# One attention block stack and one recurrent block stack in a single launch: a unit's matrices moved to memory of their own, steps reordered around them, and extra idle-time matmuls

## The chip, the cores and the metric

The kernel runs on one core of one Trainium2 chip. The metric is the device time of one execution in microseconds; the time of a kernel is the median of several runs. The profile comes from one further execution.

## The reference, cut to what matters

The program computes two transformer-like blocks in float32 on one sequence of 256 tokens and a width of 1024. The first block (two layers of three attention branches and an MLP) is not touched by the change. The second block begins with an "even mixer", which is where every edit lies:

```
q, k, v = silu(conv(x @ w_in))            # gated delta rule: 4 heads of 128
g, beta = gates(x @ w_in)
o  = gated_delta_chunked(q, k, v, g[0], beta[0]) + flip(gated_delta_chunked(flip(q), ...))
y_dn = rms_norm(o, dn_norm) * silu(dn_gate)

r, k, v, w_f, w_b, a = ...                # RWKV-7: 8 heads of 64
y  = rwkv7_scan(r, w_f, k, v, -kk, kk * a) + flip(rwkv7_scan(flip(...)))
y_rk = (group_norm(y) * ln_w + ln_b + bonus) * silu(rk_gate)

h = layer_norm(ALPHA * h + concat(y_dn, y_rk) @ w_out, ln_g, ln_b)
h = h + sigmoid(h @ ple_gate) * rms_norm(p @ ple_w, ple_norm)
```

Both recurrences are computed in chunks of 128 tokens in the kernel. A chunk needs a triangular inverse, three dependent products with it ("solve"), and a state that is handed to the next chunk; each recurrence runs once forward and once backward.

## The kernel before, in words

Each engine has a program written out by hand, and the functions of one stage are named after it: `..._tensor` runs on PE, `..._vector` on DVE, `..._scalar` on ACT, `..._gpsimd` on POOL, `..._sync` on SP, which issues all loads. Within an engine the order is the order of the calls. Engines wait for named events (`("xt", tag, i)`); an event that an engine has passed is not waited for again.

Dense products take weights in pieces of 128 x 2048. SP loads a piece, ACT rounds it (`high_of_next`, two instructions at L353), DVE makes the remainder (`low_of_next`, two instructions at L366), and PE multiplies three times (L390, L391, L392). A `Filler` is a list of steps from another stage, of which one is put between two steps of the current one.

The gated delta rule (`delta_tensor`, `delta_vector`, `delta_scalar`) goes over both directions d and in each over two chunks (step 0 and 1). A step is: kS (L2087, needs the state), the right-hand side on DVE, three solve products (L2192) with an ACT copy after the first and the second (L3195) and a DVE subtraction after the third (L2665), then o and kU or qS (L2087). `claim(..., warm=n)` takes a PSUM bank and puts n products of the identity with itself (L281, two instructions each) ahead of the wait for the operands; they compute nothing that is used.

RWKV runs as four units: (d, step) = (0,0), (0,1), (1,0), (1,1), called unit 0 to 3 here. In the text of the code, the pass n of `rwkv_tensor` and its sisters finishes the inverse of unit n-1 while it makes the matrices of unit n. The matrices are eight products for pairs of heads (`matrices_tensor`, L2395), masked on DVE into `M` (`masked_vector`, L3049). The inverse of a unit goes through: rows of the diagonal blocks (L2138 on PE, copied by ACT at L3145), substitution on DVE (L2621 and L2624), two levels of nx, rest, next_xt and turned (L2150 on PE, L2647 and L2641 on DVE, L3151 on ACT), "between" and "corner" (L2150, copied by ACT at L3159 and L3169), and `spread` (L2655). Then a unit sums (`a_sums_tensor`, L2418 and L2420; `o_values_tensor`, L2433 and L2435, into a bank of its own that `summed_vector` at L3062 and L3064 frees), solves (L2192), adds the solved part (`o_solved_tensor`, L2445) and, for step 0, makes the new state (L2457 and L2458). PSUM has eight banks, used in turn; in the RWKV part seven, with the eighth for o.

The matrices of the second unit, `self.M[1]`, lie in memory where the delta rule had its own arrays and, with their last 480 words, where the RWKV's r lies. The function `rwkv_decay_vector(k, e, 1)` is the last reader of r (L3028, L3037), and its ACT part is `decay_scalar(k, e, 1)` (L3398, L3401, L3402: exponentials of the decay sums). The delta rule's gate `silu_dn` is read last at L2735, in `normed_delta_vector`. POOL makes the decayed keys of the backward direction (`decayed_keys_gpsimd`, L3429, two instructions), which the matrices of unit 2 need.

After the last unit the output is normed per head (`normed_heads_vector`, L2980 to L3005), token tile 1 first, turned by PE (L468, copied by ACT at L477 and DVE at L487), and multiplied with `w_out_2` (four pieces), token tile 1 first.

## Time and profile before

| what | value |
|---|---|
| median of 3 runs | 1630.14 us (1622.62 to 1634.23) |
| the profiled execution: its own time, its span | 1632.06 us, 1630.8 us |
| PE busy in the span | 1528.2 us, 94% |
| DVE busy | 1059.9 us, 65% |
| ACT busy | 776.4 us, 48% |
| the mean clock that PE was granted | 0.951 of full |
| the chain that ended last | PE 78%, DVE 12%, ACT 7% |

The stage of the change lies at about 1040 to 1320 us of the span. A row of the timeline gives the start, the duration, the engine, the line of the code, the operation, and in brackets how long the engine stood idle before it and what ended that.

### The profile page before, as it was taken

The numbers are of one execution on the slowest core, as the hardware profiler recorded it, in microseconds if no ns is written. First come the engines' busy times: TensorE is split into PE (matmuls) and PEld (weight loads), VectorE is DVE, ScalarE is ACT, GpSimd is POOL, SyncE is SP. The second block draws the span as 40 slices with busy tenths as digits, with TensorE's granted clock in tenths as the row PEclk, the third lists the DMA queues.
The fourth block names the chain that finished last, engine by engine and source line by source line (L and its number), as shares of the span: only waits on it lengthen the run. The fifth ranks groups of instructions, "written<-read, shape, count | busy, mean of one in ns | idle before, by whom it ended". The sixth has DMA issues, their size and how long they took to land.

```text
span 1630.8 us, 27392 instructions
## 1 busy us (share of the span) xinstructions
PE 1528.2 (94%) x11764; PEld 1347.5 (83%) x11764; DVE 1059.9 (65%) x1828; ACT 776.4 (48%) x1316; POOL 55.0 (3%) x60
## 2 busy tenths in 40 slices
PE   7998999999999998989999999896889889999998
PEld 7888888899989898988999899885678877886566
DVE  5576656655564776566555685757366568987876
ACT  4656445544454465445444566323232326646435
POOL 0001011000000010110000000000010000000000
PEclk9999999999999999999999999987769789999999
DMA  8554344555646543444655654200001156532133
GB/s 275 179 170 130 104 152 149 178 197 191 196 130 199 186 130 110 128 153 142 204 194 182 204 164 129 79 1 2 1 2 48 60 196 181 151 110 65 52 123 129
DMA packets 151189, 219.12 MB, mean 134 GB/s; under 512 B 6228, under 2 KB 110684, under 8 KB 150428
## 3 DMA queue, kind: packets, MB, share of 16 engines
q1 hardware_dynamic: 151068, 217.37, 41.4%
q8 instruction: 92, 1.51, 0.4%
q14 instruction: 29, 0.24, 0.0%
HBM read 216.29 MB, written 1.06 MB: 133 GB/s over the span
## 4 chain that ended last, share of the span: by engine, by line
PE 78%; DVE 12%; ACT 7%; DMA 1%; issue 1%; SPq 0%; DVEq 0%; ACTq 0%
PE bank L390 20%; PE bank L392 19%; PE bank L391 19%; DVE weights_low L366 4%; PE bank L3668 2%; PE bank L2087 2%; PE bank L2192 2%; ACT weights_high L353 2%; PE bank L892 1%; PE bank L2150 1%; PE bank L3629 1%; PE bank L3678 1%; DMA place<-w_in_dram 1%; PE bank L3689 1%; PE bank L2445 1%
## 5 line engine op out<-in xcount | busy, mean ns | idle before, releaser
L366 DVE TENSOR_TENSOR weights_low<-place,weights_high 128x1024 fp32r<-128x1024 f32 (+2 forms) x387 | 449.2, 1205 | 169.8 <-ACT weights_high L353 169.2
L353 ACT ACTIVATE weights_high<-place 128x1024 fp32r<-128x1024 f32 (+2 forms) x387 | 379.0, 1033 | 125.8 <-DMA place<-w_down_dram 40.7
L390 PE MATMUL bank<-hT_high,weights_high 128*128 128x256 f32 x1152 | 330.6, 287 | 2.4 <-DVE hT_low L487 1.4
L391 PE MATMUL bank<-hT_low,weights_high 128*128 128x256 f32 x1152 | 325.0, 282 | 0.0
L392 PE MATMUL bank<-hT_high,weights_low 128*128 128x256 f32 x1152 | 324.9, 282 | 0.0
L390 PEld LDWEIGHTS bank<-hT_high,weights_high 128*128 128x128 f32 x1152 | 219.0, 190 | 6.3 <-DVE hT_low L487 2.2
L391 PEld LDWEIGHTS bank<-hT_low,weights_high 128*128 128x128 f32 x1152 | 219.1, 190 | 0.7
L392 PEld LDWEIGHTS bank<-hT_high,weights_low 128*128 128x128 f32 x1152 | 219.0, 190 | 0.0
L392 PE MATMUL bank<-weights_high,branchT_low 128*128 128x512 f32 x256 | 100.6, 393 | 0.0
L390 PE MATMUL bank<-weights_high,branchT_high 128*128 128x512 f32 x256 | 100.3, 392 | 0.3
L391 PE MATMUL bank<-weights_low,branchT_high 128*128 128x512 f32 x256 | 100.0, 390 | 0.0
L1551 ACT ACTIVATE place<-place,place 128x256 f32<-128x256 f32 x40 | 20.5, 512 | 111.9 <-DVE place L1238 111.0
L1352 DVE TENSOR_TENSOR place<-place 128x512 f32<-128x512 f32 x32 | 22.2, 693 | 69.8 <-ACT place L1617 69.8
L1617 ACT ACTIVATE place<-bank 128x512 f32<-128x512 f32 x32 | 19.2, 599 | 96.5 <-PE bank L392 96.5
L390 PE MATMUL bank<-weights_high,hT_high 128*128 128x512 f32 (+1 forms) x160 | 62.2, 389 | 2.0 <-DVE place L1049 1.2
L392 PE MATMUL bank<-weights_high,hT_low 128*128 128x512 f32 (+1 forms) x160 | 62.2, 389 | 0.0
L390 PE MATMUL bank<-hT_even_high,weights_high 128*128 128x256 f32 x208 | 60.8, 292 | 1.4 <-DVE hT_even_low L487 1.3
L391 PE MATMUL bank<-weights_low,hT_high 128*128 128x512 f32 (+1 forms) x160 | 61.6, 385 | 0.0
L390 PE MATMUL bank<-branchT_high,weights_high 128*128 128x256 f32 x192 | 57.2, 298 | 4.4 <-ACT place L1528 2.5
L392 PE MATMUL bank<-hT_even_high,weights_low 128*128 128x256 f32 x208 | 59.2, 285 | 0.0
L391 PE MATMUL bank<-hT_even_low,weights_high 128*128 128x256 f32 x208 | 59.1, 284 | 0.0
L390 PEld LDWEIGHTS bank<-weights_high,branchT_high 128*128 128x128 f32 x256 | 48.1, 188 | 10.7 <-DVE branchT_low L1354 1.1
(440 smaller groups left out, 3185.5 us busy)
## 6 DMA issues: line engine op xcount, KB each, us to landing
place<-w_in_dram SPq DMA_DIRECT2D x48, 1024.0 KB, 5.4
place<-w_up_dram SPq DMA_DIRECT2D x32, 1024.0 KB, 5.3
place<-w_down_dram SPq DMA_DIRECT2D x32, 1024.0 KB, 4.9
place<-even_w_in_dram SPq DMA_DIRECT2D x17, 1024.0 KB, 5.2
place<-w_out_dram SPq DMA_DIRECT2D x16, 1024.0 KB, 5.1
place<-odd_w_in_dram SPq DMA_DIRECT2D x16, 1024.0 KB, 5.7
place<-w_branch_dram SPq DMA_DIRECT2D x12, 1024.0 KB, 5.1
place<-ple_gate_dram SPq DMA_DIRECT2D x8, 1024.0 KB, 5.7
```

The lines of the kernel that those rows point to most:

```text
L353: nc.scalar.activation(high[:, lo:hi], self.raw[p % SLOTS][:, lo:hi], ACT.Copy).then_inc(*A("high", p, j))
L366: nc.vector.tensor_tensor(low[:, lo:hi], self.raw[p % SLOTS][:, lo:hi], high[:, lo:hi].bitcast(FP32), ALU.subtract).then_inc(*V())
L390: nc.tensor.matmul(out, left[0], right[0], start=first, stop=False)
L391: nc.tensor.matmul(out, left[0], right[1], start=False, stop=False)
L392: return nc.tensor.matmul(out, left[1], right[0], start=False, stop=last)
L892: ins = nc.tensor.matmul(banks[n][:, at_:at_ + keys], qT[:, q0:q0 + P], kT[:, 0:keys], start=j == 0, stop=j == len(pairs) - 1)
L1352: nc.vector.tensor_tensor(f.u[j], f.u[j], f.u[j], ALU.mult).then_inc(*V("squared_u", l, i, j))
L1551: nc.scalar.activation(s[:, 0:S], s[:, 0:S], ACT.Exp, bias=st[:, 0:1], accum_out=st[:, 2:3]).then_inc(*A())
L1617: nc.scalar.activation(f.u[j], split(k.bank("up", l, i, j), 2, S), ACT.Relu).then_inc(*A("relu", l, i, j))
L2087: ins = nc.tensor.matmul(b[:, h * P:(h + 1) * P], left(h), right(h), start=True, stop=True)
L2192: ins = nc.tensor.matmul(b[out, i * width:(i + 1) * width], left(u, rows), right[rows, i, :], start=True, stop=True)
L3668: ins = nc.tensor.matmul(b, left[:, tile, t, :], o.mag[n][hf][:, 0 if real else 1, t, :], start=t == 0, stop=t == TT - 1)
```

## The change

Nothing that is computed changes. The edits are:

1. Memory. `silu_dn` and `g_beta` change places among the delta rule's arrays. `whole`, an array of the first inverse, moves to where `loraT` lies. With that `M[1]` starts 512 words lower and ends before r. In exchange `silu_dn` now lies under the decayed keys that POOL writes, so POOL waits for the new event `("delta_gated", 0)` of L2735.
2. Pass n = 1. The matrices of unit 1 are masked from the first level on, one pair in each of four places, where before the last four heads came after `decay`. DVE's decay step moves behind the blocks and `compact` of unit 1, ahead of its substitution. Of ACT's decay step, the first part (two big exponentials) moves ahead of the squares of the delta norm, the second behind the copies of "corner" and "quads". On PE `o_values` goes ahead of "corner".
3. Pass n = 3. `a_sums` and its copy on ACT go ahead of "between", and `o_values` ahead of "corner".
4. Pass n = 4, the last. One piece of `w_out_2` gets its low half after the first "rest" of the inverse, a second one after `summed_vector`, a third one after the norm of token tile 1; before, two came in the middle of that norm and two after the last solve. ACT makes the high halves of the third piece after the first next_xt copy, and the square root of that norm goes ahead of the copy of "corner".
5. Extra warm products in the delta rule.

```
-        arT, self.v_rk, dbT, dkT, whole = take(4, 2, S), take(TT, WB), take(4, S), take(4, S), take(8 * 2 * QUAD)
-        self.M = [... for at in (m_at, body_at + 5 * 2 * WB + 8 * 2 * QUAD)]
+        arT, self.v_rk, dbT, dkT = take(4, 2, S), take(TT, WB), take(4, S), take(4, S)
+        whole = k.words_at(body_at + rk_words + 3 * 4 * S, 8 * 2 * QUAD)
+        self.M = [... for at in (m_at, body_at + 5 * 2 * WB)]
...
-            four_tensor(k, ("kS", *tag), ..., warm=0 if d else 2)
+            four_tensor(k, ("kS", *tag), ..., warm=2)
-                     warm=((0, 0, 0), (9, 0, 0), (3, 2, 0), (7, 2, 0))[step + 2 * d])
-        four_tensor(k, ("o", *tag), ..., ("solved", *tag, 2))
+                     warm=((0, 0, 0), (9, 3, 3), (3, 3, 3), (9, 2, 0))[step + 2 * d])
+        four_tensor(k, ("o", *tag), ..., ("solved", *tag, 2), warm=3 if step or d else 0)
-            four_tensor(k, ("kU", *tag), ..., warm=0 if d else 5)
+            four_tensor(k, ("kU", *tag), ..., warm=5)
...
 (rwkv_tensor)
-            if not more:
+            if n > 2:
                 a_sums_tensor(k, e, n - 1)
             between_tensor(k, v, tag, tag[1])
-            if more:
+            if n == 2:
                 pairs[n].finish()
                 corner_tensor(k, v, tag, tag[1])
-                if n > 1:
-                    a_sums_tensor(k, e, n - 1)
+                a_sums_tensor(k, e, n - 1)
                 o_values_tensor(k, e, n - 1)
             else:
                 o_values_tensor(k, e, n - 1)
...
 (rwkv_vector)
+                if i == 0 and not more:
+                    k.low_of_next()
                 if i == 0 and stateful:
                     summed_vector(k, e, n - 2)
-                elif more and n > 1:
+                    if not more:
+                        k.low_of_next()
+                elif more:
                     pairs[n]()
...
-            for _ in decay:
-                pass
...
                 next(normed[1])
-                k.low_up_to(("w_out_2", 0, 0, 1))
...
             compact_vector(k, unit, step_tag)
+            for _ in decay:
+                pass
             substitute_vector(k, unit, step_tag, RK_UNITS[n][0])
...
             for _ in normed[1]:
                 pass
+            k.low_of_next()
...
 (rwkv_scalar)
                     next(delta, None)
-                    next(decay, None)
-            if not more:
+                if not more and i == 0:
+                    k.high_of_next()
+            if n > 2:
                 rhs_scalar(k, e, tag)
             between_scalar(k, v, tag, tag[1])
+            if not more:
+                k.rstd_scalar(("o_rk", 1), e.stats[:, 80:88])
             corner_scalar(k, v, tag, tag[1])
...
+            if n == 1:
+                next(decay, None)
...
             rhs_scalar(k, e, step_tag)
+            next(decay)
...
 (decayed_keys_gpsimd)
-    G.wait_ge(("minus_exp", d))
+    G.wait_ge(("minus_exp", d), ("delta_gated", 0))
```

## Rows read from the trace of the kernel before

**Rows 1.** The page: the clock granted to PE in 40 slices of the span.
```profile
PEclk9999999999999999999999999987769789999999
```
**Rows 2.** The view by stretches: three low ones, the sum over eight; columns engine busy, clock, DMA.
```profile
1080.70:1091.00 10.30, 10.30 (x41) 9.07 (x41) 4.69 (x14) 4.75 (x9) 0.00 (x0) 0.50 0.00 0
...
1196.70:1224.10 27.40, 25.05 (x262) 22.75 (x261) 14.74 (x34) 6.04 (x13) 2.31 (x3) 0.50 0.01 1
1258.20:1282.10 23.90, 23.90 (x208) 22.70 (x207) 7.40 (x24) 8.84 (x14) 1.28 (x2) 0.50 0.48 177
...
sum 123.10, PE 108.90 PEld 97.76 DVE 64.42 ACT 38.32 POOL 3.59; mean PE 13.61 PEld 12.22 DVE 8.05 ACT 4.79 POOL 0.45
```
**Rows 3.** The timeline from the forward delta rule's end into the backward one.
```profile
1079.74 2.94 PE L2087 MATMUL bank<-place,place 128*128 128x128 f32 x16 [0.78 <-DVE place L2665]
...
1083.27 3.78 PE L2312 MATMUL bank<-place,place 64*128 64x256 f32 x8
...
1091.96 1.06 ACT L3270 ACTIVATE place<-place 128x1024 f32<-128x1024 f32 x1 [2.64 <-DVE place L2789]
...
1096.20 1.72 PE L281 MATMUL bank<-place 128*128 128x128 f32 x14
```
**Rows 4.** The timeline of the backward delta rule's two steps.
```profile
1151.62 1.65 PE L281 MATMUL bank<-place 128*128 128x128 f32 x6
...
1164.00 1.16 PE L2087 MATMUL bank<-place,place 128*128 128x128 f32 x8 [1.48 <-DVE place L2856]
...
1167.58 2.62 PE L281 MATMUL bank<-place 128*128 128x128 f32 x14
...
1182.23 3.73 PE L2087 MATMUL bank<-place,place 128*128 128x128 f32 x16
```
**Rows 5.** The timeline of the pass n = 1, from POOL's keys to the substitution.
```profile
1192.66 5.11 POOL L3429 TENSOR_TENSOR place<-place,place 128x1024 f32<-128x1024 f32 x2 [18.36 <-ACT place L3402]
...
1194.06 1.51 DVE L2735 TENSOR_TENSOR place<-place,place 128x512 f32<-128x512 f32 x1 [0.72 <-ACT place L3187]
...
1196.35 1.71 PE L2395 MATMUL bank<-place,place 64*128 64x256 f32 x4 [3.16 <-DVE place L3049]
...
1203.27 1.76 DVE L2598 TENSOR_TENSOR place<-place,place 32x256 f32<-32x256 f32 x4
...
1206.07 3.65 PE L2138 MATMUL bank<-place,place 128*128 128x64 f32 x16 [1.47 <-DVE place L2609]
...
1210.38 0.19 DVE L2621 TENSOR_TENSOR place<-place,place 128x16 f32<-128x16 f32 x1 [4.35 <-ACT place L3145]
```
**Rows 6.** The timeline of the passes n = 2 and n = 3.
```profile
1238.80 1.95 PE L2138 MATMUL bank<-place,place 128*128 128x64 f32 x16
...
1249.61 0.75 PE L2150 MATMUL bank<-place 32*32 32x32 f32 x64
...
1256.57 0.68 DVE L3062 COPY place<-bank 128x512 f32<-128x512 f32 x1
...
1259.65 3.62 PE L2435 MATMUL bank<-place,place 128*128 128x64 f32 x16
...
1263.06 3.62 PE L2138 MATMUL bank<-place,place 128*128 128x64 f32 x16
...
1282.34 0.75 PE L2150 MATMUL bank<-place 32*32 32x32 f32 x64
```
**Rows 7.** The timeline of the last pass.
```profile
1283.55 0.45 DVE L2641 STREAM_TRANSPOSE place<-place 128x256 f32<-128x256 f32 x1 [3.75 <-ACT place L3151]
...
1291.39 4.62 DVE L366 TENSOR_TENSOR weights_low<-place,weights_high 128x1024 fp32r<-128x1024 f32 x4
...
1296.60 1.14 PE L2192 MATMUL bank<-place,place 64*64 64x64 f32 x16 [0.36 <-ACT place L3195]
...
1300.44 1.97 PE L468 MATMUL bank<-place,place 128*128 128x128 f32 x8 [2.70 <-DVE place L3005]
...
1305.93 3.67 PE L2445 MATMUL bank<-place,place 128*128 128x64 f32 x16 [0.77 <-DVE place L2665]
...
1310.79 0.63 PE L390 MATMUL bank<-weights_high,hT_even_high 128*128 128x512 f32 x1
```

More of the change, by code:

```diff
@@ L1951, in __init__ @@
         self.k_tok = take(TT, WB)
-        self.g_beta = take(2, TT, 8)
+        self.silu_dn = take(TT, WB)
         self.AT, self.NT, self.decay = take(8, P), take(8, P), take(8, P)
         self.inverse_dn = Inverse(self.NT, *inverse_places[0])
-        self.silu_dn = take(TT, WB)
+        self.g_beta = take(2, TT, 8)
         self.dn_cols = take(104)
@@ L1964, in __init__ @@
         k.top = body_at
-        arT, self.v_rk, dbT, dkT, whole = take(4, 2, S), take(TT, WB), take(4, S), take(4, S), take(8 * 2 * QUAD)
-        self.M = [split(k.words_at(at, RK_HEADS * 4 * P), RK_HEADS, 4, P) for at in (m_at, body_at + 5 * 2 * WB + 8 * 2 * QUAD)]
+        arT, self.v_rk, dbT, dkT = take(4, 2, S), take(TT, WB), take(4, S), take(4, S)
+        whole = k.words_at(body_at + rk_words + 3 * 4 * S, 8 * 2 * QUAD)
+        self.M = [split(k.words_at(at, RK_HEADS * 4 * P), RK_HEADS, 4, P) for at in (m_at, body_at + 5 * 2 * WB)]
         self.inverse_rk = [Inverse(M[:, :, 0, :], *places) for M, places in zip(self.M, ((*inverse_places[1], whole), inverse_places[0]))]
@@ L2275, in delta_tensor @@
         if step:
-            four_tensor(k, ("kS", *tag), lambda h: e.qkvT[:, 1, h, cut], state, ("state", "dn", d), warm=0 if d else 2)
+            four_tensor(k, ("kS", *tag), lambda h: e.qkvT[:, 1, h, cut], state, ("state", "dn", d), warm=2)
         fill()
@@ L2282, in delta_tensor @@
         solve_tensor(k, e.inverse_dn, tag, inv, range(4 * c, 4 * c + 4), rhs4, U4, work4, P, between, ("rhs", *tag),
-                     warm=((0, 0, 0), (9, 0, 0), (3, 2, 0), (7, 2, 0))[step + 2 * d])
-        four_tensor(k, ("o", *tag), lambda h: e.AT[:, 4 * c + h, :], lambda h: U4[:, h, :], ("solved", *tag, 2))
+                     warm=((0, 0, 0), (9, 3, 3), (3, 3, 3), (9, 2, 0))[step + 2 * d])
+        four_tensor(k, ("o", *tag), lambda h: e.AT[:, 4 * c + h, :], lambda h: U4[:, h, :], ("solved", *tag, 2), warm=3 if step or d else 0)
         if step == 0:
             fill()
-            four_tensor(k, ("kU", *tag), lambda h: e.k_tok[:, c, h * P:(h + 1) * P], lambda h: work4[:, h, :], ("tailed", *tag), warm=0 if d else 5)
+            four_tensor(k, ("kU", *tag), lambda h: e.k_tok[:, c, h * P:(h + 1) * P], lambda h: work4[:, h, :], ("tailed", *tag), warm=5)
             fill()
@@ L2734, in normed_delta_vector @@
     V.wait_ge(("delta_scaled", t))
-    nc.vector.tensor_tensor(o, o, e.silu_dn[:, t, :], ALU.mult).then_inc(*V())
+    nc.vector.tensor_tensor(o, o, e.silu_dn[:, t, :], ALU.mult).then_inc(*V("delta_gated", t))
 def delta_sums_vector(k, e):
@@ L3356, in rwkv_scalar @@
                 quads_scalar(k, unit, step_tag, ("M_masked", *step_tag))
-                if n > 1:
+                if n == 2:
                     rhs_scalar(k, e, tag)
-            else:
-                k.rstd_scalar(("o_rk", 1), e.stats[:, 80:88])
             turn = second_calls(lambda: k.turn_scalar(("mixedT", 0), e.close.hT, KT, 1))
+            if n == 1:
+                next(decay, None)
             if more:
```

## The prediction

> **What bounds the kernel now.** I read the page first. PE holds nearly the whole chain, and the clock granted to it is full almost everywhere but in slices 28 to 33 [rows 1]; that is where the change lies. The view by stretches, set on the eight stretches of half clock between 1080 and 1313 us, then says how much: 123.1 us at half clock, with PE busy in 108.9 of them [rows 2]. So in this stage three things can be bought: a shorter chain through DVE and ACT, less PE work in front of it, and the upper of the two clock levels. The price of the clock stands in one pair of rows: the rows product (L2138) takes 3.62 us at half clock and 1.95 us at full [rows 6]. The timeline then gives the order of the steps, and I walked the new order through it with the durations of before, edit by edit. 1% (16.3 us) is about what a measurement of this kernel can tell from no change.
>
> **The change part by part.**
>
> Warm products, first place (forward direction, step 1). A warm product costs 1.72/7 = 0.25 us at full clock [rows 3] and 1.65/3 = 0.55 us at half [rows 4]. Nine are added: three ahead of the second solve product, three ahead of the third, three ahead of o. PE waits there for a copy of 0.6 to 0.7 us anyway; the last of these gaps is the 0.78 us ahead of o [rows 3]. Three times 0.25 us just fill each, so I take +0.2 us. In return the engine is dense when it comes to 1080.7 us, where now the clock falls for 10.3 us [rows 2]. At full clock the pair o and qS takes about 2.1 instead of 2.94 us, the product of L2312 about 1.9 instead of 3.78 us, and the decay products that follow come some 2.5 to 3.5 us earlier. The next in line is then ACT, whose exponential at 1091.96 us now waits 2.64 us for DVE, which waited for PE [rows 3]: ACT's own two table loads and the sigmoid come just before it and let about 3.2 us through. Sum: -3.0 us; bounds +2 us (the clock falls all the same and the warm products cost) and -4 us.
>
> Warm products, second place (backward direction). In step 0 one is added ahead of the second solve product and three ahead of the third, and PE comes to both without a pause, so 4 x 0.25 = 1.0 us lies on the path. Three ahead of o add about 0.5 us, since DVE is masking then; five ahead of kU fit in the 1.48 us of idle time [rows 4]. In return the seven warm products at 1167.58 us, which ran 2.62 us at half clock [rows 4], and kS before them may run at full clock, which gives back about 1.2 us. In step 1 the two ahead of kS and the two more ahead of the first solve product fall into waits for ACT's and DVE's copies; the set of three stands ahead of o at 1182.23 us, where PE comes directly from a_sums: +0.75 to +1.6 us, of which a clock that recovers one step earlier pays the half. Sum: +1.0 us, bounds +4 and -4 us.
>
> Pass n = 1. Now PE stands 3.16 us because the banks of the first masked heads are not free, DVE comes late to the remaining masks and to L2598 at 1203.27 us, and the rows product starts at 1206.07 us [rows 5]. In the new order the two exponentials (2.2 us) run on ACT ahead of the squares, so the squares end 0.7 us later, and DVE, which waits for them in order, holds its first mask and its first turn back by some 1.8 us. Against that, four masks and 2 decay steps (together 2 x 1.29 + 3.2 us) leave the place ahead of the blocks of unit 1. The last mask ends at about 1197.8 us. Then comes the price: POOL's two multiplications (5.11 us) now start only after L2735, at about 1196.5 us, and DVE's `spread` and L2598 fall in them. The row shows what that means: L2735, 0.65 us elsewhere, took 1.51 us while POOL ran [rows 5]. With `spread` held until POOL's first one ends and L2598 until its second one ends, L2598 starts at about 1201.8 us and the rows product at about 1204.5 us: -1.5 us. Without this contention it would be -4 us. The decay steps of DVE (2.5 us) go in front of the substitution, where DVE now waits 4.35 us for the copy of the rows [rows 5]: free at half clock, some tenths at full. ACT's second exponential with its table load (2.5 us) comes ahead of the copy of the rows and ends before it is due. The wait of POOL holds nothing up: behind it are the levels of unit 1, due in the third solve, and the keys, due in pass 2. Sum: -1.5 us, bounds -5 and +0.5 us.
>
> What the Trainium skill says of this place: SBUF — State Buffer, "Who interferes with whom", has a DVE instruction with two SBUF inputs block fully against a POOL instruction that reads SBUF, whichever starts first. The long L2735 agrees, and by this rule, which speaks against the edit, the sum above is the -1.5, not the -4 us.
>
> Pass n = 3. a_sums (1.9 us at full clock) goes into a gap of 0.9 us, so "between" comes 1 us later; o_values must wait for its bank, which L3062 frees at 1257.26 us [rows 6], and "corner" waits behind it. Against that, 2.7 + 3.6 us of PE work leave the place between "corner" and the rows product. DVE has the blocks ready at about 1260.0 us, so the rows product starts at 1260.0 to 1261.2 instead of 1263.06 us [rows 6]. Sum: -2.0 us, bounds 0 and -3 us.
>
> Last pass. Two low halves (2 x 2.31 us, half of 4.62 [rows 7]) go in front of and behind `summed_vector`, where DVE waits 3.75 us before the turn and about as long before L3064: free while the clock is half there, up to +1 us if it is full. The four instructions of 4.62 us at 1291.39 us go [rows 7]. The token tile is then ready at about 1296.2 instead of 1300.4 us; what is late next is the second solve product, which ends at 1297.7 us [rows 7], 0.3 us earlier since a table load of ACT leaves its way. The turn starts at 1297.4 instead of 1300.44 us: -3.0 us. PE's idle stretch of 2.70 us ahead of it [rows 7] is gone, so I expect the clock to stay at full: turn (1.97), third solve product (about 2) and o_solved (3.67) [rows 7] then take about half, -3.6 us, and the first seven products of the output projection, 0.63 us each at half clock [rows 7], give -1.4 us. Sum: -8 us; -3.5 us if the clock falls; bounds +1 and -9 us.
>
> Sum: -3.0 + 1.0 - 1.5 - 2.0 - 8.0 = -13.5 us. The profiled execution, 1632.06 us, would become 1618.6 us. It lies 1.9 us above the median of the runs, so the median goes from 1630.14 to about 1616.6 us.
>
> **The rivals.**
>
> R1, the clock follows the old pattern. Only the chain gets shorter: -1.5 - 2 - 3.5, and the warm products in the first two places cost about 3 us: -4 us, 1626 us. For it: the long half-clock stretches have PE busy in 25.05 of 27.4 and in all of 23.9 us [rows 2], so being busy with small products does not lift the clock.
>
> R2, the clock holds in one or both of the long stretches. The part from the rows product to next_xt takes 10.8 us in unit 1 at full clock and 19.3 us in unit 2 at half [rows 6]; less the new state (2 us) that is 6.5 us for each. 1603 to 1610 us. For it: less idle time before 1258 us. Against it: PE waits for the blocks of unit 1 for some 6 us before 1204.5 us, so at most the second one.
>
> The Trainium skill, TensorE: Matmul & The Clock Gate, "What's actually happening", says that activity releases the throttle. Taken by itself this rule gives R2 in full, about 1603 us; the stretch with 23.9 of 23.9 us busy at 0.5 [rows 2] speaks against it, and so I give it little.
>
> R3, slower. 28 warm products are added, and all lie ahead of a wait on PE, in order. Where PE has no pause and the clock is half, each costs 0.55 us [rows 4], 15 us in all. With nothing gained in clock, and 7 us from the chain, that is +8 us, 1638 us. It decides from the point where more than 13 of the 28 lie on the path at half clock. Against it: five of them lie in an idle stretch of 1.48 us [rows 4] and nine in gaps of their own length.
>
> **How the numbers follow.** Forecast 0.47, R1 0.25, R2 0.23 (both stretches 0.05 of it), R3 0.05. The forecast's own range is 1611 to 1622 us. R1 and R2 together hold half of the chance, so the range of 8 in 10 takes in most of both: 1604 to 1629 us. Faster by over 1% means below 1613.8 us: R2 and a quarter of the forecast, 0.36. Slower by over 1% means above 1646.4 us, more than R3's price: 0.02. The rest is within 1%, 0.62.
>
> **What would show it.** Right: full clock at 1081 to 1091 us; no idle time of PE ahead of L2395 in pass 1, the rows product 1 to 2 us closer to the end of the delta rule, `spread` or L2598 two to four times as long as now; L2138 of unit 2 less than 6 us after its next_xt; no L366 between L2990 and L2993, and L2445 of the last unit at about 1.95 us. Wrong: the low stretch at 1081 us is still there, or warm products followed at once by real ones in most places (R3), or new half-clock stretches in the last pass because two low halves hold back the turn.

## The result, and the profile after

| | before | after |
|---|---|---|
| median of 13 runs each | 1633.55 us (1622.62 to 1636.74) | 1618.0 us (1607.88 to 1623.59) |
| ratio | | 0.9926, 95% interval 0.9903 to 0.9949 |
| profiled execution: own time, span | 1632.06, 1630.8 us | 1619.1, 1617.8 us |
| granted clock of PE, mean | 0.951 | 0.958 |

The change makes the kernel 0.74% faster by the ratio on record, some 12 us. A ratio here is not the quotient of the two medians, which lie 15.6 us (0.95%) apart. The median of before was 1630.14 us when it was taken over 3 runs; over 13 it is 1633.55 us. The ratios leave out runs more than 1.5% above the fastest of their kernel, which of all runs in this document is one of experiment 7.

First the page's row of the clock, to be held against [rows 1]:

```profile
PEclk9999999999999999999999999997769799999999
```

Slices 27 and 33 read 9 in place of 8, and slices 28 to 32 are as before: there is less time at half clock, not none. The view by stretches (stretch, its length, busy time of PE, PEld, DVE, ACT and POOL, clock, DMA) says the same in microseconds; the first line is a full-clock stretch, set over the same time as the first of [rows 2], and the sum is that of all seven low ones:

```profile
1080.70:1091.00 10.30, 10.30 (x73) 9.17 (x71) 8.45 (x22) 7.09 (x11) 0.00 (x0) 1.00 0.01 2
...
1186.80:1190.20 3.40, 3.40 (x122) 2.53 (x111) 1.90 (x5) 0.00 (x0) 0.00 (x0) 0.50 0.00 0
1197.00:1220.90 23.90, 19.60 (x189) 18.17 (x193) 12.13 (x28) 6.81 (x13) 2.58 (x3) 0.50 0.01 1
1255.00:1275.50 20.50, 20.50 (x221) 19.02 (x221) 10.94 (x26) 9.14 (x15) 1.24 (x2) 0.50 0.58 207
...
sum 95.50, PE 81.18 PEld 71.85 DVE 53.00 ACT 28.46 POOL 3.81; mean PE 11.60 PEld 10.26 DVE 7.57 ACT 4.07 POOL 0.54
```

95.5 us at half clock against 123.1 us [rows 2]. To see where the time went I cut both timelines at the same steps. The columns are the starts of that step, and what each part between two of them gained:

| step | before | after | part is shorter by |
|---|---|---|---|
| last subtraction of the forward delta rule (L2665) | 1079.00 | 1076.95 | 2.0 (no edit lies there) |
| rows product of the backward delta rule | 1107.80 | 1101.44 | A: 4.3 |
| last DVE step of the delta rule | 1186.72 | 1182.02 | B: -1.7 (longer) |
| rows product of unit 1 | 1206.07 | 1201.30 | C: 0.1 |
| rows product of unit 2 | 1238.80 | 1234.60 | D: -0.6 (longer) |
| rows product of unit 3 | 1263.06 | 1255.95 | E: 2.9 |
| output projection | 1309.36 | 1295.47 | F: 6.8 |
| end of the last instruction | 1630.76 | 1617.81 | G: -0.9 (longer) |

A is the first place of the warm products, B the second, C the pass n = 1, E the pass n = 3, F the last pass. G holds no edit. D holds one that costs nothing there: DVE's decay step, which now comes after the rows product of unit 1, is done at 1203.6 us, and DVE still waits 2.02 us for the copy of the rows. The timeline of after, from A to F:

```profile
1077.70 2.05 PE L2088 MATMUL bank<-place,place 128*128 128x128 f32 x16
...
1080.03 1.99 PE L2313 MATMUL bank<-place,place 64*128 64x256 f32 x8
...
1086.39 1.06 ACT L3274 ACTIVATE place<-place 128x1024 f32<-128x1024 f32 x1
...
1159.08 1.16 PE L2088 MATMUL bank<-place,place 128*128 128x128 f32 x8 [0.27 <-DVE place L2856]
...
1161.92 2.17 PE L281 MATMUL bank<-place 128*128 128x128 f32 x18
...
1177.34 1.59 PE L281 MATMUL bank<-place 128*128 128x128 f32 x6
...
1178.73 2.53 PE L2088 MATMUL bank<-place,place 128*128 128x128 f32 x16
...
1186.58 0.99 PE L2151 MATMUL bank<-place,place 32*32 32x32 f32 x64 [1.66 <-DVE place L2641]
1187.50 2.08 PE L2395 MATMUL bank<-place,place 64*128 64x256 f32 x8
...
1192.13 0.69 DVE L2735 TENSOR_TENSOR place<-place,place 128x512 f32<-128x512 f32 x1 [0.71 <-ACT place L3191]
...
1192.97 5.10 POOL L3437 TENSOR_TENSOR place<-place,place 128x1024 f32<-128x1024 f32 x2 [24.36 <-DVE place L2735]
...
1194.06 1.80 DVE L2655 TENSOR_TENSOR place<-place,place 128x512 f32<-128x512 f32 x1
...
1195.90 4.45 DVE L2598 TENSOR_TENSOR place<-place,place 32x256 f32<-32x256 f32 x4
...
1201.30 3.68 PE L2139 MATMUL bank<-place,place 128*128 128x64 f32 x16 [6.59 <-DVE place L2608]
...
1249.64 2.10 PE L2420 MATMUL bank<-place,place 128*128 128x64 f32 x16
...
1253.04 2.00 PE L2435 MATMUL bank<-place,place 128*128 128x64 f32 x16 [0.68 <-DVE place L3066]
...
1255.95 3.67 PE L2139 MATMUL bank<-place,place 128*128 128x64 f32 x16
...
1268.82 2.35 DVE L366 TENSOR_TENSOR weights_low<-place,weights_high 128x1024 fp32r<-128x1024 f32 x2
...
1272.66 2.35 DVE L366 TENSOR_TENSOR weights_low<-place,weights_high 128x1024 fp32r<-128x1024 f32 x2
...
1276.69 0.45 DVE L2641 STREAM_TRANSPOSE place<-place 128x256 f32<-128x256 f32 x1 [1.67 <-ACT place L3155]
...
1289.98 1.09 PE L468 MATMUL bank<-place,place 128*128 128x128 f32 x8
...
1293.66 2.00 PE L2445 MATMUL bank<-place,place 128*128 128x64 f32 x16 [1.07 <-DVE place L2665]
```

Read it in this order.

- A: o and qS take 2.05 us and L2313 1.99 us where they took 2.94 and 3.78 us [rows 3]; ACT's exponential has no idle time ahead of it.
- B: the idle time ahead of kU fell from 1.48 [rows 4] to 0.27 us, and nine warm products run in 2.17 us at full clock; but the half-clock stretch has only moved, and now the three ahead of o cost 1.59 us.
- C: L2395 no longer waits for masks. POOL runs from 1192.97 to 1198.1 us; under it `spread` (L2655) takes 1.80 us and the four L2598 take 4.45 us, against 1.76 us in [rows 5]. PE waits 6.59 us for this chain of DVE.
- E: a_sums and o_values stand ahead of the rows product, which starts 2.9 us after the start of o_values in place of 3.4 us; but it comes to the half clock again, 3.67 us.
- F: both low halves lie where DVE waited, its wait ahead of the turned blocks is 1.67 instead of 3.75 us [rows 7], and the turn runs in 1.09 instead of 1.97 us.

### The profile page after: what moved, and what is told of

Its sections match the earlier page's. It is cut to its first block, busy times and chain, and to the rows that moved or that the text cites. A ratio compares the mean times of both kernels' runs of the same rounds, so it can differ in the third digit from the quotient of the medians.

```text
span 1617.8 us, 27504 instructions
## 1 busy us (share of the span) xinstructions
PE 1521.7 (94%) x11820; PEld 1343.3 (83%) x11820; DVE 1062.2 (66%) x1828; ACT 777.5 (48%) x1318; POOL 54.9 (3%) x60
## 4 chain that ended last, share of the span: by engine, by line
PE 79%; DVE 12%; ACT 6%; DMA 1%; issue 1%; DVEq 0%; ACTq 0%
PE bank L390 20%; PE bank L392 19%; PE bank L391 19%; DVE weights_low L366 3%; PE bank L3676 2%; PE bank L892 2%; PE bank L2193 2%; PE bank L2151 1%; PE bank L2088 1%; ACT weights_high L353 1%; PE bank L3637 1%; PE bank L3686 1%; PE bank L3697 1%; PE bank L2139 1%; PE bank L2395 1%
## 5 line engine op out<-in xcount | busy, mean ns | idle before, releaser
L366 DVE TENSOR_TENSOR weights_low<-place,weights_high 128x1024 fp32r<-128x1024 f32 (+2 forms) x387 | 449.4, 1205 | 170.7 <-ACT weights_high L353 170.1
L1617 ACT ACTIVATE place<-bank 128x512 f32<-128x512 f32 x32 | 19.1, 597 | 96.4 <-PE bank L392 96.4
```

The costliest lines, as they stand in the source:

```text
L366: nc.vector.tensor_tensor(low[:, lo:hi], self.raw[p % SLOTS][:, lo:hi], high[:, lo:hi].bitcast(FP32), ALU.subtract).then_inc(*V())
L1617: nc.scalar.activation(f.u[j], split(k.bank("up", l, i, j), 2, S), ACT.Relu).then_inc(*A("relu", l, i, j))
```

## The experiments

Twelve kernels, in three groups (1 to 4, 5 to 8, 9 to 12); those of a group share their runs of the kernel before, whose medians are 1632.65, 1632.49 and 1630.79 us. For experiments 1 to 4 the quotient of the medians (0.9934, 0.995, 0.9959, 0.9933) lies below the ratio on record by 0.002 to 0.004, as much as most of these parts are worth; I go by the ratios, and the sizes of single parts in whole executions stay that uncertain. The intervals of most ratios overlap that of the kernel after (0.9903 to 0.9949); what an edit does is therefore read in its part of the timeline. The first five put one part of the change alone into the kernel before.

**1. The forward warm products alone.**
```
-  warm=((0, 0, 0), (9, 0, 0), (3, 2, 0), (7, 2, 0))[step + 2 * d])
+  warm=((0, 0, 0), (9, 3, 3), (3, 2, 0), (7, 2, 0))[step + 2 * d])
...
   four_tensor(k, ("o", *tag), ...
+              warm=3 if step and not d else 0)
```


> The kernel before with the nine warm products of the forward delta rule alone (three each ahead of the second and third solve product and of o in its step 1). Theory (the walk through the two traces, where 4.3 us are gained between the forward rule's last step and the backward rule's blocks): the half-clock stretch at 1081 to 1091 us is gone, the exponential of the backward rule comes over 3 us earlier, 3 to 5 us faster in all, ratio 0.997 to 0.9985. Rival (the gain there came from run-to-run placement of the clock, not from the warm products): ratio 1.000, and the stretch is gone or there without rule.

Measured: 1621.8 us, 12 runs, ratio 0.9954 (0.9923 to 0.9984). With the last pass it is one of the two parts whose gain is clear of noise by itself: some 7.5 us by the ratio, 4.3 us in part A of its profile. Experiment 2 below has the same 4.3 us in A without these products, so its profile does not show that they brought it.

**2. The backward warm products alone.**
```
-  four_tensor(k, ("kS", *tag), ..., warm=0 if d else 2)
+  four_tensor(k, ("kS", *tag), ..., warm=2)
...
-  warm=((0, 0, 0), (9, 0, 0), (3, 2, 0), (7, 2, 0))[step + 2 * d])
+  warm=((0, 0, 0), (9, 0, 0), (3, 3, 3), (9, 2, 0))[step + 2 * d])
...
   four_tensor(k, ("o", *tag), ...
+              warm=3 if d else 0)
...
-  four_tensor(k, ("kU", *tag), ..., warm=0 if d else 5)
+  four_tensor(k, ("kU", *tag), ..., warm=5)
```


> The kernel before with the nineteen warm products of the backward delta rule alone. Theory (they lie on PE's path; the traces show 1.7 us lost between the backward rule's blocks and its end): 1 to 3 us slower, ratio 1.0005 to 1.002. Rival (they keep the clock up through step 1 and pay for themselves): ratio under 0.999, and no half-clock stretch between the first solve product of step 1 and its o.

Measured: 1624.56 us, ratio 0.999 (0.9961 to 1.002): no difference is shown, and the interval holds the times of the theory and of the rival. The trace speaks against the rival: the half-clock stretch between the first solve product of step 1 and its o is there, 1169.7 to 1179.9 us.

**3. Pass n = 1 alone:** the memory, POOL's wait, and the new order of masks, decay and o_values (the main lines).
```
+        whole = k.words_at(body_at + rk_words + 3 * 4 * S, 8 * 2 * QUAD)
...
-                elif more and n > 1:
+                elif more:
                     pairs[n]()
...
-            for _ in decay: pass          # ahead of spread
+            for _ in decay: pass          # ahead of substitute_vector
...
-    G.wait_ge(("minus_exp", d))
+    G.wait_ge(("minus_exp", d), ("delta_gated", 0))
```


> The kernel before with the new memory of the second unit's matrices, POOL's new wait and the new order of pass 1 alone. Theory (DVE's spread and L2598 stand behind POOL's multiplications): the idle time of PE at the matrices is gone, yet the rows product comes at the same distance from the end of the delta rule as before, 0 to -1 us, ratio 0.999 to 1.0005. Rival (the order itself gains the 1.5 us that I forecast or more, and the trace of after lost it elsewhere): rows product 1.5 to 4 us closer.

Measured: 1626.0 us, ratio 0.9991 (0.9965 to 1.0016). Its timeline of the place:

```profile
1192.39 1.14 PE L2395 MATMUL bank<-place,place 64*128 64x256 f32 x8
...
1196.68 5.10 POOL L3431 TENSOR_TENSOR place<-place,place 128x1024 f32<-128x1024 f32 x2 [21.90 <-DVE place L2735]
...
1199.61 4.45 DVE L2598 TENSOR_TENSOR place<-place,place 32x256 f32<-32x256 f32 x4
```

L2395 runs at full clock here, 1.14 us, and part C is 1.5 us shorter than before. In the whole change the same product took 2.08 us and C gained 0.1 us. By its trace the edit works as the prediction said, which is the edge of the rival above and not the 0 to 1 us that I had put on record for this run; the ratio, whose interval holds 1, can't tell. In the change's own profile a half-clock stretch of 3.4 us at 1186.8 us eats it. Experiments 7 and 8 have such a stretch in the same place (from 1187.2 and 1187.7 us) and also gain nothing in C.

**4. The last pass alone.**
```
+                if i == 0 and not more:
+                    k.low_of_next()
                 if i == 0 and stateful:
                     summed_vector(k, e, n - 2)
+                    if not more:
+                        k.low_of_next()
...
-                k.low_up_to(("w_out_2", 0, 0, 1))
...
+            k.low_of_next()
             last = lambda: k.turn_vector(...)
...
+                if not more and i == 0:
+                    k.high_of_next()
+            if not more:
+                k.rstd_scalar(("o_rk", 1), e.stats[:, 80:88])
```


> The kernel before with the new places of the low halves and of the square root in the last pass alone. Theory: the turn no longer waits for the norm, the solve runs through at full clock, 6 to 8 us between next_xt of the last pass and the output projection's first product, 5 to 7 us in the median, ratio 0.9955 to 0.997. Rival (only 3 us of chain are gained here and the rest was a lucky clock): ratio 0.998, with a half-clock stretch over the third solve product.

Measured: 1621.75 us, ratio 0.996 (0.993 to 0.999); part F is 6.0 us shorter. The half-clock stretch over the third solve product is gone, as the theory says. The other kernels bear it out: all five without this edit (before, 1, 2, 3, 5) have 13.7 us at half clock over the end of the last pass (1299.2 to 1312.8 us in the kernel before), and of the nine with it eight have 3.4 us there and one none.

**5. Pass n = 3 alone.**
```
-            if not more:
+            if n > 2:
                 a_sums_tensor(k, e, n - 1)
             between_tensor(k, v, tag, tag[1])
...          (o_values ahead of corner; the copy on ACT likewise)
```


> The kernel before with a_sums ahead of between and o_values ahead of corner in pass 3 alone. Theory: the rows product of unit 3 starts 2 to 3 us closer to the masks, with the half-clock stretch still there, ratio 0.998 to 0.999. Rival (the denser PE keeps the clock up): 6 to 9 us, ratio under 0.996.

Measured: 1631.13 us against 1632.49 us, ratio 0.9993 (0.9971 to 1.0015); part E is 2.3 us shorter, too little to show in the ratio; the stretch over the rows product is still there, 20.5 us long.

The next three change the kernel after.

**6. POOL early.** The first token tile of `silu_dn` gets words of its own, so POOL need not wait for L2735.
```
+        self.silu_dn = Tiles(k.words_at(free_words, WB), k.words_at(silu_at + WB, WB))
-    G.wait_ge(("minus_exp", d), ("delta_gated", 0))
+    G.wait_ge(("minus_exp", d), ("delta_gated", 1))
```
(`delta_gated` 1 is the tile that is gated first, 13 us earlier.)

> The changed kernel with the first tile of the delta gate in 512 free words past the other arrays, so that POOL's key multiplications need not wait for that gate and run some 9 us earlier. Theory (they hold up spread and L2598): spread back to 0.7 us, the four L2598 to 1.8 us, the rows product of unit 1 about 3.5 us earlier, 3 to 4 us faster than the changed kernel. Rival (DVE was slowed by something else, ACT's long queue for instance): rows product unchanged.

Measured: 1613.83 us (1608.73 to 1620.03), ratio 0.9907 (0.9873 to 0.9942). Its timeline:

```profile
1187.26 4.65 POOL L3448 TENSOR_TENSOR place<-place,place 128x1024 f32<-128x1024 f32 x2 [14.86 <-ACT place L3421]
...
1188.39 1.25 DVE L2740 TENSOR_SCALAR place<-place 128x4 f32<-128x4 f32 x1 [1.55 <-ACT place L3194]
...
1199.13 0.68 DVE L2666 TENSOR_TENSOR place<-place,place 128x512 f32<-128x512 f32 x1
1199.84 1.76 DVE L2609 TENSOR_TENSOR place<-place,place 32x256 f32<-32x256 f32 x4
...
1202.56 2.13 PE L2150 MATMUL bank<-place,place 128*128 128x64 f32 x16 [1.81 <-DVE place L2619]
```

With POOL gone from under them, `spread` is back at 0.68 us (from 1.80) and the four products at 1.76 us (from 4.45): 3.8 us of contention, shown by taking it away. Part C is 2.6 us shorter than before, 2.5 us shorter than in the kernel after. Some of the rest is given back at once: POOL now runs under the delta norm and holds L2740, an instruction on four columns, for 1.25 us. The median is 4.2 us below that of the kernel after, but the two intervals overlap.

**7. 22 warm products ahead of unit 1's rows product.**
```
-        rows_tensor(k, e, then, following)
+        rows_tensor(k, e, then, following, warm=22 if n == 0 else 0)
```


> The changed kernel with 22 warm products ahead of the rows product of unit 1, in the 6.6 us in which PE waits. Theory (idle time there drops the clock, and small products do not bring it back): no half-clock stretch from the rows product to the new state, 5 to 7 us faster than the changed kernel. Rival (the clock falls for what the products after it are, not for the idle time ahead): stretch still there, and up to 6 us slower because the warm products run at half clock.

Measured: 1624.42 us, 12 runs, ratio 0.9958 (0.9934 to 0.9982). Without the longest (1645.43 us) the other eleven lie between 1615.6 and 1632.36 us, 16.8 us apart, the widest spread of the changed kernels. The median is 6.4 us above that of the kernel after, though the two intervals overlap. Yet its profile, which is of its fastest run, looks like a full success:

```profile
1195.03 5.18 PE L281 MATMUL bank<-place 128*128 128x128 f32 x44
...
1201.70 2.00 PE L2139 MATMUL bank<-place,place 128*128 128x64 f32 x16 [1.49 <-DVE place L2608]
```

The 22 fill the wait, the rows product runs at full clock, and part D is 7.3 us shorter. The same 22 at half clock take 22 x 0.55 = 12 us [rows 4], 5 to 6 us more than the wait that hides them. The four longest executions, above 1629 us, have a mean clock of 0.953 and less, the four below 1620 us have 0.960 and more; that the long ones are those in which the clock was already down at the products is argued from this, no trace of one exists.

**8. Three warm products ahead of the third unit's o_values.**
```
-    b = k.claim("o", *tag, bank=O_BANK)
+    b = k.claim("o", *tag, bank=O_BANK, warm=3 if n == 2 else 0)
```


> The changed kernel with three warm products ahead of o_values in pass 3, in PE's wait of 0.68 us. Theory (PE's work there is just too thin): no half-clock stretch from 1255 to 1275 us, 5 to 7 us faster than the changed kernel. Rival: the stretch stays, no change within 1 us.

Measured: 1611.92 us (1609.25 to 1615.06), ratio 0.989 (0.9865 to 0.9916). Its timeline:

```profile
1253.28 0.68 DVE L3066 COPY place<-bank 128x512 f32<-128x512 f32 x1
...
1254.01 0.94 PE L281 MATMUL bank<-place 128*128 128x128 f32 x6 [0.78 <-DVE place L3066]
...
1254.78 1.90 PE L2435 MATMUL bank<-place,place 128*128 128x64 f32 x16
...
1257.23 2.00 PE L2139 MATMUL bank<-place,place 128*128 128x64 f32 x16
...
1259.16 1.15 PE L2193 MATMUL bank<-place,place 64*64 64x64 f32 x32
...
1265.19 0.74 PE L2151 MATMUL bank<-place,place 32*32 32x32 f32 x64 [1.18 <-DVE place L2641]
```

Three products and a half-clock stretch of 6.8 us (1266.3 to 1273.1), where the kernel after has 20.5 us over rows product and solve. Part F is 10.7 us shorter than before, against 6.8 us in the kernel after. This is the cheapest edit of the study.

They don't fill the wait, as I had meant them to. `claim` waits for the bank before it issues them, so PE still stands 0.78 us, until L3066 has freed the bank at 1253.96 us; the three come behind that wait and put o_values off by 0.77 us. What differs from the kernel after is thus 0.8 us more of PE work ahead of o_values, not less idle time. Nor are they the only thing that shortens this stretch: it is 10.2 us long in experiments 3 and 6, which don't have them, and 20.5 to 23.9 us in the other eight without them.

The last four, with the kernel after as the base again, ask which of these add up.

**9. The kernel after without the 19 backward warm products.** The reverse of the diff of experiment 2.

> The kernel after without the 19 added warming products of the backward delta rule; the 9 of the forward one stay. Theory (those 19 only lengthen PE's list there, by 1.8 us in all runs that had them, whatever the clock did): from the start of the backward rows to the end of the delta rule 1.8 us less than the kernel after, median about 1616 us, ratio to the kernel before 0.991. Rival (they keep the clock up for what follows): a half-clock stretch returns between the backward rows and the solve in this profile, and the median is 2 us or more above the kernel after, ratio above 0.995.

Measured: 1612.52 us (1607.01 to 1618.7), ratio 0.990 (0.9868 to 0.9933). Part B is back to that of before (-0.1 us; the kernel after has +1.7 us), although it has 3.2 us more at half clock than the kernel after. By the trace the theory stands, and the median is below the 1616 us that it gave, but the interval overlaps that of the kernel after. The rival had one thing right, a stretch of 3.4 us that comes in B (1161.1 to 1164.5 us), but it costs less than the 19 products.

**10. All three: experiments 6, 8 and 9 together.**

> The kernel after without the backward warming products, with the second delta gate's words off the tile that GpSimd reads beside VectorE (as in the run with the early GpSimd products), and with 3 warming products ahead of the output matmuls of the third unit. If the three add: 1.8 us from the first, 3 us from the second, 5 us from the third, so about 1609 us, ratio 0.986. Rival (they draw on the same thing, the clock in the two long stretches, and each has it or not by where PE's gaps fall): no better than the run with the 3 warming products alone, 1612 us, ratio 0.989.

Measured: 1609.0 us (1604.32 to 1614.51), ratio 0.9881 (0.9849 to 0.9912). The time is the one expected of the sum, but the interval holds both its 0.986 and the rival's 0.989, so whether the three add is not decided. Beside experiment 12, the same kernel without the edit for POOL (0.9884), that edit adds nothing that can be measured.

**11. Experiments 8 and 9, with 8 warm products ahead of unit 1's rows product.**

> The next kernel (no backward warming, 3 products ahead of the third unit's output matmuls) with 8 warming products ahead of the second unit's rows product in place of the 22 tried before. Theory (22 cost 11 us where the clock is already at half, 8 fit in the wait of 6 us even then, so the bad executions go and the good ones stay): the spread shrinks to some 8 us and the median is 2 to 5 us under the kernel without them, about 1607 us. Rival (8 are too few to raise the clock where it has fallen before): the rows product stands at 3.2 us or more in the profile as in the kernel after and the median is within 1 us of the kernel without them.

Measured: 1610.27 us (1607.11 to 1613.39), ratio 0.9886 (0.9854 to 0.9918). The rows product stands between the two theories:

```profile
1194.46 2.05 PE L281 MATMUL bank<-place 128*128 128x128 f32 x16
...
1200.24 2.65 PE L2139 MATMUL bank<-place,place 128*128 128x64 f32 x16 [3.72 <-DVE place L2608]
```

The eight take 2.05 us and then PE waits 3.72 us, the clock falls at 1201.4 us, and the median is that of the kernel without them. So eight do no harm and no good. That the spread is small is no credit of theirs: experiment 12 has a smaller one.

**12. Experiments 8 and 9 together.**

> The kernel after without the backward warming products and with 3 warming products ahead of the third unit's output matmuls: the common base of the two runs before it. Theory (both edits act in places of their own): 1.8 us under the run with those 3 products alone (1611.9 us), so about 1610 us, ratio 0.988. Rival (moving what lies behind the delta rule by 1.8 us changes where the clock falls): the half-clock stretch over the third unit's rows product is back, rows product 3.6 us, median about 1616 us.

Measured: 1609.74 us (1607.89 to 1612.37), ratio 0.9884 (0.9855 to 0.9912). The trace goes against the rival: the third unit's rows product keeps its 2.00 us, F its 10.7 us:

```profile
1201.06 3.68 PE L2139 MATMUL bank<-place,place 128*128 128x64 f32 x16 [6.30 <-DVE place L2608]
...
1247.22 0.94 PE L281 MATMUL bank<-place 128*128 128x128 f32 x6 [0.78 <-DVE place L3066]
...
1250.44 2.00 PE L2139 MATMUL bank<-place,place 128*128 128x64 f32 x16
```

It is the version to keep: 1.16% faster than the kernel before, by 19 products less and 3 more than the kernel after. Experiment 10, which has the memory edit on top, is the same by its ratio (0.9881), though its one profile has the shortest span of all (1603.0 us).

**All of them side by side.** Change of each part against the kernel before (us, one profile each), and in brackets the time at half clock within the part:

| kernel | A | B | C | D | E | F | G |
|---|---|---|---|---|---|---|---|
| before, length | 28.8 (10.2) | 78.9 (47.8) | 19.3 (9.3) | 32.7 (18.0) | 24.3 (4.9) | 46.3 (29.2) | 321.4 (7.4) |
| after | -4.3 (0) | +1.7 (44.3) | -0.1 (7.7) | +0.6 (19.6) | -2.9 (0.9) | -6.8 (19.6) | +0.9 (14.6) |
| 1 | -4.3 (0) | -2.4 (41.1) | 0.0 (9.4) | -0.2 (17.9) | -0.3 (4.4) | +0.1 (29.3) | +0.3 (7.7) |
| 2 | -4.3 (0) | -0.5 (40.9) | 0.0 (11.0) | -5.2 (6.1) | -0.1 (4.8) | -0.5 (28.7) | +0.5 (7.9) |
| 3 | +0.9 (12.9) | 0.0 (47.8) | -1.5 (4.3) | +0.7 (19.6) | -0.9 (3.1) | -5.3 (17.1) | +0.7 (11.5) |
| 4 | -1.1 (6.8) | -0.1 (47.6) | +0.1 (9.1) | +0.2 (18.3) | -0.2 (4.6) | -6.0 (19.8) | -3.2 (4.2) |
| 5 | +0.7 (12.4) | 0.0 (47.8) | 0.0 (9.5) | -3.9 (7.6) | -2.3 (2.2) | -0.5 (28.7) | -2.9 (4.5) |
| 6 | -2.7 (3.4) | +1.8 (44.3) | -2.6 (6.9) | -5.3 (3.4) | +1.2 (10.1) | -11.3 (7.7) | -2.8 (4.5) |
| 7 | -4.3 (0) | -0.6 (37.6) | 0.0 (3.4) | -7.3 (0) | +1.7 (11.1) | -5.1 (20.7) | -1.3 (6.0) |
| 8 | -4.3 (0) | -0.6 (37.5) | -0.1 (7.8) | +0.6 (19.6) | -2.6 (0) | -10.7 (6.8) | -2.1 (8.0) |
| 9 | -2.7 (3.4) | -0.1 (47.5) | -1.5 (4.2) | -5.0 (6.2) | -2.2 (2.6) | -6.8 (19.0) | -1.5 (5.9) |
| 10 | -4.3 (0) | -1.9 (37.5) | -3.9 (3.4) | -4.8 (6.8) | -2.6 (0) | -10.7 (6.8) | -1.2 (3.4) |
| 11 | -4.3 (0) | -2.1 (41.0) | -0.9 (3.4) | -0.6 (17.1) | -2.6 (0) | -10.7 (6.9) | -2.1 (8.1) |
| 12 | -2.7 (3.4) | -0.1 (47.5) | -1.5 (4.3) | -5.0 (6.3) | -2.6 (0) | -10.7 (6.9) | +3.0 (13.8) |

Two readings. Down column D, in which no edit that costs time lies but that of experiments 7 and 11, the time goes with the bracket: 19.6 us at half clock give +0.6 or +0.7, 6 to 8 us give about -5, none gives -7.3; that is 0.4 us for each microsecond at half clock. Column G, without an edit, goes the same way, less closely: 3.4 to 6 us at half clock give -1.2 to -3.2 us, 11.5 us and more give +0.7 to +3.0. In D the time goes with the bracket even in kernels whose code for that part is the same (before and 5; after, 6 and 9). So one profile shows the part's own edit and, on top, a draw of the clock worth up to 6 us (D without experiment 7 runs from -5.3 to +0.7). In experiment 3 it gives F 5.3 us that no edit of its own made: the stretch in front of F is 10.2 us long there in place of 23.9. Column A makes the same point against the change: experiment 2, without forward warm products, has the same -4.3 us as the kernels with them. At equal clock, none of it half, the nine products thus cost nothing. Column B can be read at equal clock. With 44 us at half clock the kernels with the backward warm products (after, 6) stand at +1.7 and +1.8 us, and even with 47.5 us those without them (3, 4, 5, 9, 12) stand at 0.0 or -0.1; with 41 us it is -0.5 (2) against -2.4 and -2.1 (1, 11); with 37.5 us -0.6 (7, 8) against -1.9 (10). The 19 products cost 1.3 to 1.9 us at every clock.

## Why the prediction was right

It said 1616.6 us, from 13.5 us off a profiled execution of 1632.06 us; the profile gave 1619.1 us, 13.0 us off, and the median is 1618.0 us. It was right because the large terms were, and because the errors of the small ones and a gain that no edit made cancelled; that it comes within 0.5 us is luck, since executions of the kernel after alone differ by 16 us. Much of the gain is clock: the mean granted clocks of 0.951 and 0.958 stand for some 160 and 136 us at half clock in the whole span, and at 0.4 us each that is 9 to 10 of the 13 us, some of it counted on in the terms for A and F.

- **Warm products, first place, -3.0 us: right in kind, a little small.** The clock holds at 1081 us and A gained 4.3 us; ACT lets more through than the 3.2 us that I had allowed (its exponential comes 3.5 us earlier against the start of A). How much of it is owed to the nine products is less clear than the profile of after makes it look. Of the five profiles without them (before, 2 to 5) four have 6.8 to 12.9 us at half clock in A and one none; of the nine with them six have none and three have 3.4 us. So they make the fall rarer and shorter, they don't exclude it. The ratio of experiment 1 puts them at -7.5 us with an interval of -12.6 to -2.6.
- **Warm products, second place, +1.0 us: right in sign, too small, and the most useful step to have doubted further.** Measured +1.7 us in B; experiment 9, which only takes them out, gives 1.8 us back in the same part. The four in step 0 cost what I had said, and the three ahead of o at half clock 1.59 us, my upper price. What failed is the return: the stretch at half clock moved from 1176.3 to 1169.7 us and kept its length of 10.2 us. Column B shows that this is the rule: at any clock they cost 1.3 us or more.
- **Pass n = 1, -1.5 us: the mechanism right, and its size as well, but not in the kernel after.** `spread` held to 1.80 us and L2598 to 4.45 us are the contention I had put in; C is -1.5 us in experiments 3, 9 and 12. In the profile of after, 3.4 us at half clock after PE's wait of 1.66 us took it all (C is -0.1 us). Experiment 10 reaches -3.9 us, close to what I had put for no contention, yet not without it: POOL still holds L2740 there, for 0.89 us. The rule of the Trainium skill, SBUF — State Buffer, "Who interferes with whom", which I weighed there, holds: with POOL's reads elsewhere, both DVE steps with two SBUF inputs fall back to 0.68 and 1.76 us.
- **Pass n = 3, -2.0 us: right,** -2.9 us in the profile of after and -2.3 us alone, and by the mechanism that was said. DVE has the blocks ready 21.2 us after the rows product of unit 2 in both kernels (1260.05 us before, 1255.79 us after); PE came to them 3.0 us late and now comes 0.2 us late.
- **Last pass, -8 us: right to its parts.** From the rows product to the turn 37.4 us became 34.0 us: -3.35 us where -3.0 was said. From the turn to the projection 8.9 us became 5.5 us: -3.4 us where -3.6 was said. The -1.4 us of the projection's first products did not come, as the clock fell at 1296.0 us for 3.4 us; from the third of them on they stand at 0.63 us, as in [rows 7]. Both halves go with the edit: the front of F has as much half clock as before (19.5 us against 19.1), and the end of F lost its stretch in every kernel with the edit (experiment 4).
- **What I had not in the sum:** -2.0 us ahead of the stage, where nothing is changed, and +0.6 and +0.9 us in D and G. D and G go with the clock, which has 1.6 and 7.2 us more at half. Ahead of the stage it has 3.4 us less, which is at most a part of the 2.0 us; the rest is open.
- **The signs.** Full clock at 1081 to 1091 us, no idle time ahead of L2395, the longer `spread` and L2598, no L366 inside the norm and L2445 of the last unit at full clock all came. L2138 less than 6 us after its next_xt was missed by little (6.2 us in E, 9.1 us before). The rows product of unit 1 closer to the end of the delta rule did not come (0.1 us).

**The rivals.** R1 (the clock keeps its old pattern, 1626 us) is refuted for A and F and true for D and the front of F: the two long stretches are still there, 23.9 and 20.5 us long. R3 is refuted in its size: 19 of the 28 cost 1.8 us in all, and the other nine gain. Experiment 7, with 22 in one wait and a median 6 us above that of the kernel after, is what one would see if its mechanism were real. R2 (the clock holds in a long stretch, 1603 to 1610 us) didn't happen by the change, yet experiments 8 and 12 brought it about, and it gave 3.9 us in F where I had put 6.5. My reason against it, that PE is busy throughout these stretches and the clock stays down all the same, was true of what happens inside one; it says nothing on what starts it. With three products more between the wait for the bank and o_values the second stretch is 6.8 us long in all four kernels that have them (8, 10, 11, 12), and 10.2 to 23.9 us in the ten that don't.

On this the Trainium skill, TensorE: Matmul & The Clock Gate, "What's actually happening", which I gave little weight as its rule taken alone gave 1603 us, came out half right: activity put ahead of the fall goes with a clock that stays up (experiment 8), while 20.5 us of a PE that is busy all the time at 0.50 (the view by stretches above) did not bring it back.

**What stays open.** The five parts measured alone give ratios of 0.9954, 0.999, 0.9991, 0.996 and 0.9993, together -1.1%, against -0.74% for all at once; by the quotients of the medians it is -2.3% against -0.95%. Each ratio has an interval of 0.2 to 0.3% to either side, and the first four share their runs of before, so no interaction is shown by this; nor is it excluded. Open too is what makes the clock fall where it does: every part was traced once for each kernel.

## What to carry to other kernels

Where the place at which the clock falls is worth more than the edits, one profile of a kernel is one draw: cut the timelines of several kernels at the same steps, write the time at half clock beside each part, and credit an edit only with what its part shows at equal clock. Try a few matmuls just ahead of a dense stretch (three, behind a wait of 0.78 us, came with 3.9 us less in F); weigh a larger set with its price at half clock. Look in the trace on which side of a wait they run: those behind the wait for the bank do not fill it. When arrays are moved to share words, look at what the new wait makes coincide: here POOL's two multiplications were moved on top of the DVE steps that set the path, for 3.8 us.

## What the runs showed of the hardware that I had not expected

- Three products, 0.8 us of PE work behind an idle time of 0.78 us that stays, go with nearly 14 us less of a half-clock stretch (experiment 8 against after: 6.8 and 20.5 us).
- Executions of one and the same program differ by 16 us with the mean granted clock: the kernel after took 1607.88 us at 0.968 and 1623.59 us at 0.955. The kernel before spreads by 22 us (1616.69 to 1638.36 us in the group of experiment 1). With the three warm products six executions lie within 4.5 us in experiment 12 (0.963 to 0.966), but within 10.2 us in experiment 10.
- POOL's multiplication holds not only large DVE instructions: L2740, on 128 x 4 with one input, took 1.25 us under it in experiment 6 and 0.17 us without.
- A stretch of half clock costs some 0.4 us per microsecond here (column D), nearly what it costs a product that is all PE: the rows product takes 3.62 us at half clock and 1.95 us at full, 0.46 us per microsecond.
